# A hybrid trunk step with 16 experts: first expert's routing by halves, four split pairs, some low halves on GpSimd

## What is computed

```python
def _expert_choice_ffn(h, p):
    cap = CAPACITY_FACTOR * S // N_EXPERTS            # 64 of 512, 16 of 128
    aff = jax.nn.softmax(logits, axis=-1)
    gate, idx = lax.top_k(aff.transpose(0, 2, 1), cap)
    xs = jax.vmap(lambda hb, ib: hb[ib])(h, idx)
    gg = jnp.einsum('becd,edf->becf', xs, p['w_e_gate'])
    uu = jnp.einsum('becd,edf->becf', xs, p['w_e_up'])
    y = jnp.einsum('becf,efd->becd', jax.nn.silu(gg) * uu, p['w_e_down']) * gate[..., None]
    return ...                                        # y added into the rows idx
```

## Time and profile before

| | us |
|---|---|
| median of 3 runs | 1223.4 |
| lowest and highest | 1223.13, 1223.48 |
| span of the profiled execution, first to last instruction | 1217.1 |
| TensorE busy in it | 1176.7 (97%) |
| VectorE busy | 907.2 (75%) |
| ScalarE busy | 616.9 (51%) |
| GpSimd busy | 283.4 (23%) |

### The profile page before, as it was taken

One profiled execution on the slowest core, in us unless ns is written; L12 is line 12 of the kernel. 1 busy time (PEld: TensorE's weight loads), 2 busy tenths in 40 slices (PEclk: granted clock), 3 DMA queues, 4 the chain that ended last, 5 costly groups with the idle time before them and its releaser, 6 DMA issues.

```text
span 1217.1 us, 18950 instructions
## 1 busy us (share of the span) xinstructions
PE 1176.7 (97%) x7392; PEld 943.8 (78%) x7392; DVE 907.2 (75%) x1056; ACT 616.9 (51%) x710; POOL 283.4 (23%) x189
## 2 busy tenths in 40 slices
PE   4899999999999999999999999999999999999995
PEld 3798899988899999999995666666666666666663
DVE  2699665558777175237559999999999999999996
ACT  3421232235551251322125777777777777777783
POOL 1041030003201143333125112222222112222213
PEclk9999999999999999999999999999999999999997
DMA  9986727230212122444349999999999999999995
GB/s 320 309 233 208 249 80 168 70 108 24 87 36 95 44 71 88 170 160 147 116 172 357 387 379 378 378 379 381 381 386 390 380 378 378 379 381 380 381 364 194
DMA packets 158859, 303.27 MB, mean 249 GB/s; under 512 B 7363, under 2 KB 63719, under 8 KB 158802
## 3 DMA queue, kind: packets, MB, share of 16 engines
q1 hardware_dynamic: 145894, 271.23, 62.2%
q0 software_dynamic: 3968, 12.64, 4.7%
q10 hardware_dynamic: 8940, 18.58, 4.3%
HBM read 285.25 MB, written 17.18 MB: 248 GB/s over the span
## 4 chain that ended last, share of the span: by engine, by line
PE 90%; DMA 4%; DVE 2%; issue 1%; ACT 1%; POOL 1%; SPq 1%; POOLq 0%; DVEq 0%; ACTq 0%
PE bank L1769 17%; PE bank L1770 16%; PE bank L1771 16%; PE bank L1795 6%; PE bank L1800 5%; PE bank L1797 5%; PE bank L1798 5%; PE bank L1799 5%; PE bank L1796 5%; DMA wring<-in_w_ada 2%; PE bank L1827 1%; PE bank L2052 1%; PE bank L2035 1%; DMA scratch_acc<-ye,idx_s 1%; PE bank L2025 1%
## 5 line engine op out<-in xcount | busy, mean ns | idle before, releaser
L1769 PE MATMUL bank<-h2r_a,xTh 128*80 128x512 f32 x376 | 148.3, 394 | 0.0
L1771 PE MATMUL bank<-h2r_a,xTl 128*80 128x512 f32 x376 | 146.4, 389 | 0.0
L668 POOL TENSOR_TENSOR half<-half 1x1 f32<-1x1 f32 x26 | 60.2, 2315 | 287.8 <-DVE ye L1734 286.7
L1770 PE MATMUL bank<-l2r_b,xTh 128*80 128x512 f32 x316 | 124.2, 393 | 0.0
L1204 DVE SCALAR_TENSOR_TENSOR fa<-fa,cwT 128x655 f32<-128x655 f32 x120 | 116.6, 1001 | 1.4
L1032 ACT CAST h2r_a<-w_a 128x2048 fp32r<-128x2048 f32 x46 | 88.0, 1913 | 39.7 <-PE bank L1771 39.7
L1795 PE MATMUL bank<-hTh,hring 128*128 128x320 f32 x320 | 104.4, 326 | 3.7 <-DVE lring L1187 2.7
L565 POOL TENSOR_TENSOR lring<-wring,hring 128x2048 fp32r<-128x2048 f32 x15 | 70.1, 4675 | 161.7 <-ACT hring L727 161.7
L1800 PE MATMUL bank<-hTh,lring 128*128 128x320 f32 x320 | 98.8, 309 | 0.0
L1798 PE MATMUL bank<-hTl,hring 128*128 128x320 f32 x320 | 98.8, 309 | 0.0
L1797 PE MATMUL bank<-hTl,hring 128*128 128x320 f32 x320 | 98.8, 309 | 0.0
(11 more groups left out here) (425 smaller groups left out, 3246.9 us busy)
## 6 DMA issues: line engine op xcount, KB each, us to landing
w_b<-in_w_e_down SPq DMA_DIRECT2D x48, 1024.0 KB, 14.9
w_e<-in_w_e_up SPq DMA_DIRECT2D x32, 1024.0 KB, 16.8
w_r<-in_w_e_gate SPq DMA_DIRECT2D x32, 1024.0 KB, 17.6
w_a<-in_w_e_gate SPq DMA_DIRECT2D x32, 1024.0 KB, 14.8
w_a<-in_w_e_up SPq DMA_DIRECT2D x32, 1024.0 KB, 14.1
wring<-in_w_in SPq DMA_DIRECT2D x20, 1024.0 KB, 5.3
w_a<-in_w_e_down SPq DMA_DIRECT2D x16, 1024.0 KB, 14.1
fa<-in_w_ada SPq DMA_DIRECT2D x14, 1024.0 KB, 9.9
```

The source lines that it names most:

```text
L1769: pe.matmul(out, lh, rh, start=start, stop=False)
L1770: pe.matmul(out, lh, rl, start=False, stop=False)
L1771: return pe.matmul(out, ll, rh, start=False, stop=stop)
```

## The change

It has these parts, all around the experts.

1. **Softmax and `rstd2` order.** GpSimd computes the last tile's factor (`rstd2(4)`) ahead of `scaled(4)`; before it was the other way round. `hot_p` becomes a tensor_tensor with the rank broadcast instead of a tensor_scalar.
2. **The 0/1 matrix in two batches.** Ranks of tiles 1 and 3, then their half of `hot`; ranks of 2 and 4, then theirs. TensorE's gathering matmuls go batch by batch, both banks in each.
3. **Rows turned and cast by halves.** ScalarE makes both copies to `parts`; TensorE turns each half once its copy is there; unit 0 waits for the first half of `x_lo` alone, unit 1 for the second. `x_lo(0)` stands after search round 0 instead of before round 4. The warm-up matmuls around this are gone, and the small list matmuls (`first_lists`) move ahead of unit 1, `turn_lists` ahead of unit 5.
4. **Four split pairs.** `h2r_c` and `l2r_c` are added (the final buffers move by 256 columns); the pair is k % 4, and cast k waits for unit k - 4.
5. **Low halves.** GpSimd makes those of units 0, 2, 3, 5, 8 of expert 0 and that of unit 6 of each later expert; VectorE makes the rest (low 1 of expert 0 just after `hot`, low 4 before search round 4). There are two semaphores now, one for each maker. Low 0 of expert 0 no longer waits for `hot`.
6. **Smaller moves.** ScalarE casts unit 0 and unit 1 before the stores of the tiles, unit 3 right after `x_hi(0)`; its function table for Silu is loaded after that. SyncE has expert 1 written out and loads `final_norm_g` behind all the weights, where ScalarE loaded it at 653.62. Some semaphores of the early part are merged.

```diff
-LISTS_AT = (4, 0)
+LISTS_AT = (5, 0)
+POOL_FIRST, POOL_REST = (0, 2, 3, 5, 8), (6,)
...
-            return h2r[k % 3], l2r[k % 3]
+            return h2r[k % 4], l2r[k % 4]
...
-            for i in range(3, TT):
-                scaled(i)
-                rstd2(i)
+            scaled(3)
+            rstd2(3)
+            rstd2(4)
+            scaled(4)
...
-            gp.wait_ge(s_idx, 2)
-            first_lo(0)
-            gp.wait_ge(s_gx, 1)
+            expert_lo(0, 0)
+            gp.wait_ge(s_gx, 2)
             for b in range(4):
                 gp.wait_ge(s_hst[b], 32 if b == 0 else 16)
-            first_lo(1)
-            first_lo(2)
+            for k in POOL_FIRST[1:-1]:
+                expert_lo(0, k)
...
-            def expert(e, last):
-                if not last:
-                    gp.wait_ge(e_xt, 2 * e + 2)
-                    gather(e + 1)
+            def expert(e):
+                gp.wait_ge(e_xt, 2 * e + 2)
+                gather(e + 1)
+                for k in (POOL_FIRST[-1:] if isinstance(e, int) and e == 0 else POOL_REST):
+                    expert_lo(e, k)
...
-                    act.wait_ge(e_unit, 12 * e + (k - 2))
+                    act.wait_ge(e_unit, UNIT_N * e + (k - 3))
...
-            dve.tensor_scalar(hot_p, slot_n[:, 0:CAP_P], rank[:, 0:1], None, ALU.is_equal).then_inc(s_idx, 1)
-            for i in range(TT - 1):
-                ranks(1 + i, bank[0], P * i)
-            link(dve.tensor_reduce(rank[:, 1:TT], above[:, 1:TT, :], AX, ALU.add))
-            dve.tensor_tensor(hot, slot_n.unsqueeze(1).to_broadcast([P, TT - 1, CAP_S]),
-                              rank[:, 1:TT].unsqueeze(2).to_broadcast([P, TT - 1, CAP_S]), ALU.is_equal).then_inc(s_idx, 1)
+            dve.tensor_tensor(hot_p, slot_n[:, 0:CAP_P], rank[:, 0:1].to_broadcast([P, CAP_P]), ALU.is_equal).then_inc(s_idx, 1)
+            for b in range(2):
+                for i in (b, b + 2):
+                    ranks(1 + i, bank[0], P * i)
+                link(dve.tensor_reduce(rank[:, 1 + b:TT:2], above[:, 1 + b:TT:2, :], AX, ALU.add))
+                dve.tensor_tensor(hot[:, b:TT - 1:2, :], slot_n.unsqueeze(1).to_broadcast([P, 2, CAP_S]),
+                                  rank[:, 1 + b:TT:2].unsqueeze(2).to_broadcast([P, 2, CAP_S]), ALU.is_equal).then_inc(s_idx, 1)
+            dve.wait_ge(s_h2p, 2)
+            e_lo_unit(0, 1)
...
-            warm(WARM_B)
-            pe.wait_ge(s_gs, 2)
-            for c in range(DC):
-                x0 = (c % 4) * M_E
...
+            for hf in range(2):
+                pe.wait_ge(s_gs, hf + 1)
```

More of the change, by code:

```diff
@@ L110, with lo_made @@
 EXPERT_UNITS += [("w_e_down", None, q) for q in range(4)]
+UNIT_N = len(EXPERT_UNITS)
+POOL_FIRST, POOL_REST = (0, 2, 3, 5, 8), (6,)
+def lo_made(e, k):
+    first = isinstance(e, int) and e == 0
+    pool = POOL_FIRST if first else POOL_REST
+    by_pool = sum(x <= k for x in pool)
+    if k in pool:
+        return "pool", by_pool if first else len(POOL_REST) * (e - 1) + (len(POOL_FIRST) + by_pool)
+    return "dve", k + 1 - by_pool if first else (UNIT_N - len(POOL_REST)) * (e - 1) + (UNIT_N - len(POOL_FIRST) + k + 1 - by_pool)
 def expert_unit(k):
@@ L439, in split_of, with expert_lo_ready @@
                 return [x[:, :] for x in (hl6, hl7, hl8)[k - 6]]
-            return h2r[k % 3], l2r[k % 3]
+            if isinstance(e, int) and e == E_N - 1 and k >= 4:
+                h, low = {4: (0, 0), 5: (1, 2), 9: (2, 3), 10: (0, 0), 11: (1, 2)}[k]
+                return h2r[h], l2r[low]
+            return h2r[k % 4], l2r[k % 4]
+        def expert_lo_ready(eng, e, k):
+            by, n = lo_made(e, k)
+            eng.wait_ge(e_lop if by == "pool" else e_lod, n)
         def split(u):
@@ L515, in expert @@
                     src = a[name][0, at(e), rows, cols].rearrange("o (c p) n -> p (o c) n", p=P)
-                    if not (isinstance(e, int) and e == 0):
-                        sp.wait_ge(e_lo, 12 * e + (k - 11))
+                    if not first:
+                        expert_lo_ready(sp, e - 1, k)
                     elif k < 2:
@@ L528, in expert @@
                         sp.wait_ge(s_nm, 2)
-                        sp.wait_ge(s_gx, 1)
+                        sp.wait_ge(s_gx, 2)
                     sp.dma_start(w2[k].rearrange("p (c n) -> p c n", n=src.shape[2]), src).then_inc(e_w[k], 16)
             expert(0)
-            with sp.Fori(1, E_N) as e:
+            expert(1)
+            with sp.Fori(2, E_N) as e:
                 expert(e)
+            sp.wait_ge(e_unit, UNIT_N * (E_N - 1) + 4)
+            sp.dma_start(fgbc, a["final_norm_g"].rearrange("(o d) -> o d", o=1).to_broadcast([P, D])).then_inc(s_fg, 16)
             sp.wait_ge(e_add, 16 * (E_N - 1))
@@ L692, in _ @@
             gp.wait_ge(s_xst, 16 * TT)
-            expert(0, False)
+            expert(0)
             with gp.Fori(1, E_N - 2) as e:
-                expert(e, False)
-            expert(E_N - 2, False)
+                expert(e)
+            expert(E_N - 2)
+            for k in POOL_REST:
+                expert_lo(E_N - 1, k)
             gp.wait_ge(e_add, 16 * (E_N - 1))
@@ L1085, in _ @@
             store_x(4)
+            e_hi_unit(0, 0)
             store_h(4)
-            e_hi_unit(0, 0)
+            e_hi_unit(0, 1)
             store_h(3)
-            for k in (1, 2):
-                e_hi_unit(0, k)
-            act.activation(stat[0:1, 51:52], ident[0:1, 0:1], ACT.Silu)
-            act.wait_ge(s_gx, 1)
-            act.copy(parts[:, 0:512], bank[4][:, :]).then_inc(s_gs, 1)
+            e_hi_unit(0, 2)
+            for hf in range(2):
+                act.wait_ge(s_gx, hf + 1)
+                act.copy(parts[:, 512 * hf:512 * hf + 512], bank[4 + hf][:, :]).then_inc(s_gs, 1)
             def x_hi(n):
@@ L1627, in _ @@
             for r in range(CAP_S // 8 - 1):
-                if r == 3:
-                    dve.wait_ge(s_gx, 1)
-                    dve.tensor_copy(parts[:, 512:1024], bank[5][:, :]).then_inc(s_gs, 1)
+                if r == 1:
+                    x_lo(0)
                 if r == 4:
-                    x_lo(0)
+                    e_lo_unit(0, 4)
+                if r == 6:
                     dve.wait_ge(s_idxp, 1)
@@ L1698, in expert @@
                 first = isinstance(e, int) and e == 0
-                e_lo_unit(e, 4)
-                e_lo_unit(e, 5)
+                e_lo_run(e, (5,) if first else (4, 5))
                 gated(e, 0)
@@ L1816, in _ @@
                 last = pe.transpose(bank[7][:, 2 * dc:2 * dc + 2], c2[:, dc * P:(dc + 1) * P], ident[0:2, 0:2])
-            last.then_inc(s_ct, 1)
+            last.then_inc(s_turn, 1)
             def ada(i):
@@ L2232, in _ @@
                     warm(WARM_A)
-            pe.wait_ge(s_idx, 2)
-            pe.wait_ge(s_h2p, 2)
-            for hf in range(2):
-                for i in range(2):
+            for i in range(2):
+                pe.wait_ge(s_idx, 2 + i)
+                if i == 1:
+                    pe.wait_ge(s_h2p, 2)
+                for hf in range(2):
                     for g in range(4):
@@ L2262, in turn_lists @@
                 pe.transpose(bank[7][0:CAP_P, 2 * E_N:3 * E_N], idxf[PROMPT, 0:CAP_P], ident[PROMPT, PROMPT]).then_inc(s_idxp, 1)
-            warm(WARM_C)
             def turn_tokens(e):
@@ L2287, in gate_up @@
                         turn_lists()
+                    if isinstance(e, int) and e == 0 and (k, c) == (1, 0):
+                        first_lists()
                     last = mm3(out, xTh[:, 4 * r + c, :], xTl[:, 4 * r + c, :], wh[:, c, :], wl[:, c, :],
```

121 lines of the change are left out of this document (67 added, 54 removed).

## The result

| | us |
|---|---|
| before, median of 4 runs beside it | 1223.3 |
| after, median of 4 runs (1314.2 to 1319.9) | 1315.4 |
| ratio, 95% interval | 1.0774 (1.0758 to 1.0789) |
| span of the profiled execution after | 1312.4 |

The change makes the kernel 7.7% slower, 92 us by the medians. I had forecast 1273, 50 us more, with a range up to 1284: the direction and the place were right, the size was about half.

What follows compares the result with a forecast made beforehand. TensorE was taken as the bound, busy 97% and waiting for nobody in the loop. -0.8 + 5.0 + 46.2 - 1.1 + 0.3 = +49.6 on 1217.1 gives 1266.7, plus 6.3 around it 1273 us; whole range 1218 to 1284.

Steps and rivals of the forecast that it cites:

- The place and the chain: Experts 1 to 14: GpSimd's addition waits until 11.2, low 6 runs behind low 7, TensorE waits 3.3 us before unit 6.
- the copy of indices some 0.3 where it is not blocked, the addition 0.18: GpSimd's queue between scatter and gather in each later expert: assumed lengths in us, with scatter and gather holding 0.96 each.
- ready to start at 14.2: GpSimd reaches low 6 14.2 us after unit 0, then waits for VectorE's low 7 and runs from 15.5 to 20.1.
- 14 x 3.3 = 46.2: The loop's term: experts 1 to 14 each lose 3.3 us waiting for low 6, +46.2 us.
- Rival 3: A worse phase: GpSimd reaches low 6 after low 8 started, at 18 or later; 6 to 6.6 us an expert, 1319; chance 0.1.
- Rivals 1 and 2: Milder outcomes for blocking between VectorE and GpSimd: 1227 with chance 0.1, and 1219.5 with chance 0.17.
- Turns by order of issue: Waiting addition enters after VectorE's running low half; TensorE never waits in the loop; +3.4 us, 1227; chance 0.1.
- No blocking: GpSimd's low halves run beside VectorE's, low 6 is in time, unit 0 starts at 650.2; -3.9 us, 1219.5; chance 0.17.
- The signs: Expected in the trace: 37.5 us an expert, 3.3 wait before unit 6, addition over 6, second `hot` over 2, L1508's successor over 1.
- Routing: Before expert 0: L1508's sum waits until 637.3, the second matrix batch until 649.3; unit 0 starts at 654.2, -0.8 us.
- Expert 0: List matmuls +0.7, and TensorE waits for `gated` +1.5, low 7 +0.9 and low 8 +1.9: 39.9 us, +5.0.
- The end: After the loop: `ye` of expert 14 at offset 3.3 instead of 4.4, -1.1 us; loading `final_norm_g` late, +0.3.

Runs made afterwards that it cites:

- experiment 7: The changed kernel with one wait more: in experts 1 to 14 VectorE begins low 7 only when GpSimd has made low 6; 1271.6 us, ratio 1.0414.
- experiment 6: The changed kernel with low 6 ahead of addition and scatter, one addition for scatter and gather, and index copies an expert ahead; 1232.7 us, ratio 1.0075.
- experiment 3: The changed kernel with low 6 of each later expert moved between the scatter and the index copy, addition and gather; 1243.9 us, ratio 1.0187.
- experiment 4: The changed kernel with the gather's index copied an expert ahead and one addition for scatter and gather, low 6 behind both; 1313.6 us, ratio 1.0756.
- Experiment 8: The changed kernel with 18 matmuls nobody reads, issued by TensorE before its wait for low 6 in experts 1 to 14; 1291.5 us, ratio 1.0560.
- experiment 1: The changed kernel with no low half on GpSimd after the first expert, VectorE making all twelve; 1225.9 us, ratio 1.0040.

## Why the prediction was right and wrong

- **The place and the chain: right.** One wait in each expert, before unit 6, released by GpSimd's low half. The first addition was forecast to stand until offset 11.2; it ended at 1028.65, offset 11.3. Low 7 was forecast at 13.15 and began at 13.2.
- **The step that failed: "the copy of indices some 0.3 where it is not blocked, the addition 0.18".** From the copy's start to the addition's it is 0.78 us. In experiment 7 the copy takes the same 0.70 while VectorE stands idle, so no block makes it long. It takes 0.18 in experiment 6, where the queue was idle; here it ends 0.2 us after the scatter's 1.46 are up, so I read it as finished only behind the scatter, which I had let hold the engine 0.96. That reading is argued, not tested. The sum had a slip as well: its terms as written give 12.6 for the addition and 13.9 for low 6, where I wrote 14.2, which would put the addition at 12.9. The addition came at 13.24, 0.05 us behind low 7, and GpSimd came to low 6 at 16.7 instead of "ready to start at 14.2". I let low 6 alone wait for low 7's end (15.5); in fact addition and gather had to come behind that end as well. That makes 1.2 us of low 6: the wait is 4.42 instead of 3.3. I wrote that half a microsecond in scatter or gather "changes little". Experiments 3 and 4 show what is true of it: shorter ahead of low 7 changes nothing while anything is left to fall under it, and 35.3 instead of 40.96 once low 6 is ahead.
- **The term that was missing, and the larger one: the clock.** The sum took a wait at its own length, and put what the clock takes behind it at nothing. Experiment 8 measures the rest: 2.2 us an expert, some 30 in all. It is most of what the forecast of the loop lacked: 14 x 3.3 = 46.2 was forecast, 88.1 came, and 46.2 + 14 x 1.1 + 14 x 2.3 = 93.8, less the 5.8 by which the first step is short of the others (1.0 instead of 6.8), is 88.0.
- **Rival 3** gave 6 to 6.6 us an expert, near the 6.76, and 1319. GpSimd did come to low 6 after low 8's start, by 0.14 us. But low 8 did not hold it up: it stood still itself. Low 6 began at 16.7, not at 18 or later, and that the number agrees is luck: the clock gave what the phase did not.
- **Rivals 1 and 2.** Turns by order of issue fall for a waiting GpSimd: the addition stood 6.50 us, and two lows of VectorE began after it and went first. No blocking falls with experiments 3 and 7. Their 0.27 of chance made the range wide on the wrong side.
- **The signs.** The first addition took over 6 us, and the second `hot` over 2, as named. An expert of 37.5 us did not come. GpSimd's low 6 was to start up to 1.5 us before VectorE's low 7 ends; it started 1.2 behind that end. L1508's successor was to take over 1 us and took 0.95.
- **Routing.** L1508's successor was blocked nearly as long as forecast, and the second `hot` too, 2.18:

```profile
638.21 0.95 DVE L1543 TENSOR_TENSOR fa<-fa 128x80 f32<-128x80 f32 x1
...
648.54 2.18 DVE L1657 TENSOR_TENSOR fa<-fa 128x128 f32<-128x128 f32 x1
```

 From that first row to unit 0 it is 17.1 us, 18.5 before: -1.4, where -0.4 was forecast from there (18.1, from 636.1 to 654.2). The 0.4 by which unit 0 is later in the trace came in with the start that is 1.9 later.
- **Expert 0: +5.0 forecast, +5.8 measured**, with waits at the three places that were named: 2.1 for `gated`, 0.8 before unit 7, 1.5 before unit 8. Low 4 on VectorE was blocked by GpSimd's low 3, as written.
- **The end.** -0.8 forecast, +1.0 measured. The last expert's units took 1.6 more, and they hang on its low 6 on GpSimd: in experiment 1, without it, they take what they took before. I had put it at 0.6, which TensorE was to have to spare. VectorE's low 7 stood under that low 6 (5.31 us), and TensorE waited 0.9 us before unit 8. `ye` of expert 14 came at offset 3.3, as forecast, but that it gave the 0.6 is not shown: from the last expert's last matmul to the end it is 14.4 us in the changed kernel, and the two traces of before differ there by 1.1 themselves (15.0 and 16.1). The 0.3 for `final_norm_g` is a term that no run shows.
- **"So a waiting GpSimd gets in only where VectorE has a gap, or an instruction that reads at most one SBUF tile"**: half right. In the first part GpSimd's addition did end where VectorE's run of lows ended. Seen from the other side, an addition with one operand (2.66) and a cast (3.00) stood still behind GpSimd's lows; search rounds and compares with a sum did not.

## What to carry to other kernels

When two engines block each other as here, an item's lateness comes in steps of the other engine's instruction: find what begins next there, and ask whether your item is ahead of it by more than your error; if not, take both outcomes as cases. Give the slower engine the item with the latest due time: low 9 cost nothing where low 6 cost 88 us. And price a wait on TensorE with what the clock takes behind it, by a row of this kernel's own.
